# One plain pair of feed-forward columns fewer in each of three stages, with VectorE making those units' low parts in two of them

## The reference

```python
def swiglu(x, w_gate, w_up, w_down):
    return (jax.nn.silu(x @ w_gate) * (x @ w_up)) @ w_down
h = h + 0.5 * swiglu(rmsnorm(h, norm), w_gate, w_up, w_down)   # widths 1024 -> 2816 -> 1024
```

## Time and profile before

| | |
|---|---|
| time, median of 3 | 1736.12 us (1735.33 to 1736.40) |
| profiled execution: own time / span | 1735.85 us / 1734.1 us |
| busy share of the span: PE / PEld | 99% / 85% |
| DVE / ACT / POOL | 67% / 50% / 45% |
| granted TensorE clock, mean | 0.997 |
| start of stage one / two / three on PE (first L620 of the stage) | 7.37 / 888.58 / 1372.9 us |

### The profile page before, as it was taken

How to read it: one execution, slowest core, us unless ns; L and a number is a source line. 1 busy time by engine, 2 the same in 40 slices (tenths; PEclk the granted TensorE clock), 3 DMA queues, 4 the chain that set the end, 5 groups by cost and what they waited for, 6 DMA issues and landing times.

```text
span 1734.1 us, 28483 instructions
## 1 busy us (share of the span) xinstructions
PE 1720.6 (99%) x10096; PEld 1475.9 (85%) x10096; DVE 1156.5 (67%) x1709; ACT 870.9 (50%) x1486; POOL 782.8 (45%) x423
## 2 busy tenths in 40 slices
PE   9999999999999999999999999999999999999998
PEld 7899988888888777788888999988866889999887
DVE  6887874278867885236469877743786598787532
ACT  6455552266554477785344555522425445555322
POOL 2344354467565433325453344544533534435443
PEclk9999999999999999999999999999999999999998
DMA  5333333333333221112323333333362323333332
GB/s 178 98 103 104 108 101 95 128 95 88 110 110 113 63 72 50 50 50 85 98 92 94 107 107 101 108 97 98 103 146 62 97 85 101 105 109 110 97 97 74
DMA packets 50519, 168.56 MB, mean 97 GB/s; under 512 B 6264, under 2 KB 7032, under 8 KB 50304
## 3 DMA queue, kind: packets, MB, share of 16 engines
q1 hardware_dynamic: 47088, 161.34, 31.0%
q10 hardware_dynamic: 3344, 6.05, 1.2%
HBM read 161.84 MB, written 2.11 MB: 95 GB/s over the span
## 4 chain that ended last, share of the span: by engine, by line
PE 93%; DVE 3%; issue 2%; ACT 1%; POOL 1%; DMA 0%; POOLq 0%; SPq 0%; ACTq 0%
PE bank L620 16%; PE bank L621 16%; PE bank L622 16%; PE bank L734 8%; PE bank L735 8%; PE bank L732 8%; PE bank L914 8%; PE bank L746 3%; PE bank L959 2%; PE bank L985 2%; PE bank L1087 1%; PE bank L976 1%; PE bank L744 1%; DVE input_low L1691 1%; DVE tile L1708 1%
## 5 line engine op out<-in xcount | busy, mean ns | idle before, releaser
L487 POOL TENSOR_TENSOR weights_low<-raw_weights,weights_high 128x1024 fp32r<-128x1024 f32 x192 | 470.2, 2453 | 559.5 <-ACT weights_high L1204 531.0
L1204 ACT CAST weights_high<-raw_weights 128x1024 fp32r<-128x1024 f32 x244 | 254.7, 1048 | 295.0 <-DMA raw_weights<-weights 277.2
L528 POOL TENSOR_TENSOR weights_low<-raw_weights,weights_high 128x512 fp32r<-128x512 f32 x100 | 149.5, 1516 | 285.1 <-DVE weights_low L1844 285.1
L620 PE MATMUL bank<-input_high,weights_high 128*128 128x512 f32 x624 | 246.2, 395 | 2.8 <-DVE input_low L1691 2.1
L622 PE MATMUL bank<-input_low,weights_high 128*128 128x512 f32 x624 | 243.1, 390 | 0.0
L621 PE MATMUL bank<-input_high,weights_low 128*128 128x512 f32 x624 | 243.1, 390 | 0.0
L734 PE MATMUL bank<-input_mixed,weight_sum_low 128*128 128x256 f32 x600 | 169.7, 283 | 0.0
L735 PE MATMUL bank<-input_mixed,weight_sum_high 128*128 128x256 f32 x600 | 169.6, 283 | 0.0
L732 PE MATMUL bank<-input_mixed,weight_sum_high 128*128 128x256 f32 x600 | 169.5, 282 | 0.0
L735 PE MATMUL bank<-input_mixed,weights_high 128*128 128x256 f32 x600 | 169.4, 282 | 0.0
L732 PE MATMUL bank<-input_mixed,weights_high 128*128 128x256 f32 x600 | 169.1, 282 | 0.0
(11 more groups left out here) (322 smaller groups left out, 4139.7 us busy)
## 6 DMA issues: line engine op xcount, KB each, us to landing
raw_weights<-weights SPq DMA_DIRECT2D x294, 512.0 KB, 3.6
out_t<-out_t SPq DMA_DIRECT2D x8, 256.0 KB, 2.2
residual<-x_t SPq DMA_DIRECT2D x6, 256.0 KB, 6.2
glu_stacked<-glu_padded ACTq DMA_DIRECT2D x24, 64.0 KB, 4.5
glu_stacked<-glu_padded SPq DMA_DIRECT2D x24, 64.0 KB, 4.4
mem_in<-mem_t ACTq DMA_DIRECT2D x1, 1024.0 KB, 4.8
tile<-forget_sums ACTq DMA_DIRECT2D x4, 256.0 KB, 3.3
raw_weights<-weights SPq DMA_DIRECT2D x3, 256.0 KB, 6.2
```

Of the source, the lines that this page charges most:

```text
L487: pool.tensor_tensor(wl[:, u % RING, :], raw[:, u % RING, :], wh[:, u % RING, :].bitcast(F32), ALU.subtract).then_inc(low_done, 1)
L528: pool.tensor_tensor(wl[:, u % RING, w], raw[:, u % RING, w], wh[:, u % RING, w].bitcast(F32), ALU.subtract).then_inc(low_done, 1)
L620: pe.matmul(out, wh[:, u % RING, w], rh, start=start, stop=False)
L1204: act.copy(wh[:, u % RING, :], raw[:, u % RING, :]).then_inc(high_done, 1)
```

## The change

Plain pairs go from 6, 5, 5 to 5, 4, 4, so that 17, 18 and 18 pairs are mixed. With an even number of plain pairs the mixed pairs use banks 6/7 and 0/1 in turn (`pair_bank`), so the first product need not wait for a plain pair to be emptied; the down product's first unit goes through the banks in an order that fits. In stages two and three VectorE makes the low parts of units 2 to 7 (`weight_low`), and GpSimd makes none of the plain ones. `sums` is issued inside the first pair, two chunks before its end, and the factor is spread one chunk earlier. The seven combinations of the input are stored in another order, and for chunks 2 and 3 they are rounded and subtracted in two pieces (the first 3, then the last 4); the first product waits for the first pieces, the wide product of the first mixed pair for the last ones. ScalarE's order loses the two `high`s and the `silu` of the pair that is gone. TURN_1S is only renamed.

```diff
-PLAINS = {"g1": 6, "g2": 5, "g3": 5}
+PLAINS = {"g1": 5, "g2": 4, "g3": 4}
+EARLY, LATE = slice(0, 3), slice(3, 7)
-ND_OF, E_OF, NF_OF, NG_OF, B21, B22, B11, B12 = range(8)
+B11, E_OF, NG_OF, B21, ND_OF, B22, NF_OF, B12 = range(8)
...
+        def pair_bank(name, p):
+            n = PLAINS[name]
+            return 2 * ((n + p) % 2) if n % 2 else 6 * (p % 2 == 0)
...
 # GpSimd, gate_up_lows
-                for u in range(first, u0 + 2 * plain):
+                for u in range(first, 0 if u0 else 2 * plain):
                     low_part(u)
                 next_quarter(0)
...
 # TensorE, pair_start: in the loop over k, not behind it
-                if name != "ffn1":
-                    sums(name)
+                    if k == (DK if name in ("ffn2", "ffn3") else DK + 2) and name != "ffn1":
+                        sums(name)
 # TensorE, gate_up
-                    project(u0 + 2, ..., inside=lambda: spread_factor(feed), behind=1)
+                    project(u0 + 2, ..., inside=lambda: spread_factor(feed), behind=0)
 # TensorE, first_product
-                pe.wait_ge(sem("xmix_low"), before(name, 4) + 4)
-                pe.wait_ge(sem("ff_hidden"), before(name, FC) + plain - 1)
+                pe.wait_ge(sem("xmix_low"), before(name, 6) + 4)
+                if plain % 2:
+                    pe.wait_ge(sem("ff_hidden"), before(name, FC) + plain - 1)
                 pe.wait_ge(sem("quarter_low"), pairs_before(name, 1) + 1)
 # TensorE, mixed_pair, ahead of wide_product
+                if p == 0:
+                    pe.wait_ge(sem("xmix_low"), before(name, 6) + 6)
 # ScalarE, gate_up, stages two and three
                     high(u0 + 7)
-                    mixed_input(2)
-                    if plain > 4:
-                        high(u0 + 8)
-                    mixed_input(3)
+                    mixed_input(2, EARLY)
+                    mixed_input(2, LATE)
+                    mixed_input(3, EARLY)
+                    mixed_input(3, LATE)
                     silu(2)
-                    if plain > 4:
-                        high(u0 + 9)
-                        silu(3)
 # VectorE
+            def weight_low(u):
+                dve.wait_ge(high_done, u + 1)
+                dve.tensor_tensor(wl[:, u % RING, :], raw[:, u % RING, :], wh[:, u % RING, :].bitcast(F32),
+                                  ALU.subtract).then_inc(low_done, 1)
 # VectorE, factor(name, u0)
                     total_squares(name)
+                if u0:
+                    weight_low(u0 + 2)
                 inverse(name)
+                if u0:
+                    weight_low(u0 + 3)
 # VectorE, gate_up, the order of stages two and three after it
+                    plain_taken(0)        mixed_input(0)
+                    weight_low(u0 + 4)    plain_hidden(0)    mixed_input(1)
+                    weight_low(u0 + 5)    mixed_input_low(0, 1)
+                    plain_taken(1)        plain_hidden(1)    mixed_input(2)
+                    weight_low(u0 + 6)    mixed_input_low(1, 2)
+                    mixed_input(3)        weight_low(u0 + 7)
+                    mixed_input_low(2, 3, EARLY)    mixed_input_low(3, 5, EARLY)
+                    mixed_input_low(2, 5, LATE)     mixed_input_low(3, 6, LATE)
+                    plain_taken(2)        frame(-1)          plain_hidden(2)
+                    plain_taken(3)        plain_hidden(3)
 # VectorE, the order of stage one after plain_hidden(1), mixed_input(2), mixed_input_low(1)
+                    plain_taken(2)    mixed_input(3)
+                    the same four pieces of mixed_input_low
+                    plain_hidden(2)   plain_taken(3)    plain_hidden(3)   frame(-1)

```

More of the change, by code:

```diff
@@ L711, in gate_up @@
                 else:
-                    project(u0 + 2, bank[2][:, :], xh, xl, u0 + 3, inside=lambda: spread_factor(feed), behind=1)
+                    project(u0 + 2, bank[2][:, :], xh, xl, u0 + 3, inside=lambda: spread_factor(feed), behind=0)
                     project(u0 + 3, bank[3][:, :], xh, xl, u0 + 4)
@@ L766, in mixed_pair @@
                 plain, mixed = PLAINS[name], FC - PLAINS[name]
-                up, gate, b = u % RING, (u + 1) % RING, 2 * ((plain + p) % 2)
+                up, gate, b, after = u % RING, (u + 1) % RING, pair_bank(name, p), pair_bank(name, p + 1)
                 first, second = slice(0, HALF), slice(HALF, S)
@@ L786, in mixed_pair @@
                     pe.wait_ge(sem("ff_hidden"), at(before(name, FC) + plain + p, 1))
-                    mixed_product(bank[2 - b][:, first], wh[:, (u + 2) % RING, 0:S], quarter_low, B11
+                    mixed_product(bank[after][:, first], wh[:, (u + 2) % RING, 0:S], quarter_low, B11
                                   ).then_inc(sem("products"), 1)
@@ L800, in down @@
                     spread_unit(u0 + f, hidden_high(f), hidden_low(f), u0 + f + 1,
-                                first=(4, 5, 6, 7, 0, 1, 2, 3) if f == 0 else (), held=(0, "ff_hidden", before(name, FC) + FC))
+                                first=() if f else (4, 5, 6, 7, 0, 1, 2, 3) if PLAINS[name] % 2 else (2, 3, 4, 5, 6, 7, 0, 1),
+                                held=(0, "ff_hidden", before(name, FC) + FC))
                 with pe.Fori(0, 2) as i:
@@ L1325, in silu, with mixed_input @@
                     act.activation(tiles[c % 2][:, :], tiles[c % 2][:, :], ACT.Silu).then_inc(sem("ff_silu"), 1)
-                def mixed_input(k):
+                def mixed_input(k, part=slice(0, 7)):
                     act.wait_ge(sem("xmix_made"), before(name, 4) + k + 1)
-                    act.copy(xmix[k][:, :, 0:HALF], xsum[k % 3][:, 0:7, :]).then_inc(sem("xmix_high"), 1)
+                    act.copy(xmix[k][:, part, 0:HALF], xsum[k % 3][:, part, :]).then_inc(sem("xmix_high"), 1)
                 def copy_product(dst, src, at):
@@ L1344, in at @@
                         return n if i is None else i * (2 * step) + n
-                    b = bank[2 * ((plain + p) % 2)]
+                    b = bank[pair_bank(name, p)]
                     act.wait_ge(unit_done, at(u0 + 2 * (plain + p) + 2, 2))
@@ L1410, in gate_up @@
                     high(8)
-                    mixed_input(2)
+                    mixed_input(2, EARLY)
                     high(9)
+                    mixed_input(2, LATE)
+                    mixed_input(3, EARLY)
+                    mixed_input(3, LATE)
                     silu(2)
-                    high(10)
-                    mixed_input(3)
                     silu(3)
-                    high(11)
-                    silu(4)
                 frame(-1)
-                copy_product(copies[:, 0, 0, :], bank[2 * (plain % 2)][:, 0:HALF], 1)
+                copy_product(copies[:, 0, 0, :], bank[pair_bank(name, 0)][:, 0:HALF], 1)
                 silu(plain - 1)
@@ L1857, in gate_up @@
                 mixed_input(0)
-                if not u0:
-                    plain_taken(1)
-                plain_hidden(0)
-                mixed_input(1)
-                mixed_input_low(0)
-                if u0:
-                    plain_taken(1)
-                plain_hidden(1)
-                mixed_input(2)
-                mixed_input_low(1)
-                if not u0:
-                    plain_taken(2)
-                mixed_input(3)
-                if u0:
-                    plain_taken(2)
@@ L1873, in gate_up @@
-                mixed_input_low(2)
-                plain_hidden(2)
-                if not u0:
-                    plain_taken(3)
-                mixed_input_low(3)
-                if not u0:
-                    plain_hidden(3)
-                for c in range(3 if u0 else 4, plain - 1):
-                    plain_taken(c)
-                    plain_hidden(c)
-                frame(-1)
+                if u0:
+                    weight_low(u0 + 4)
+                    plain_hidden(0)
+                    mixed_input(1)
+                    weight_low(u0 + 5)
+                    mixed_input_low(0, 1)
+                    plain_taken(1)
+                    plain_hidden(1)
+                    mixed_input(2)
+                    weight_low(u0 + 6)
+                    mixed_input_low(1, 2)
+                    mixed_input(3)
+                    weight_low(u0 + 7)
+                    mixed_input_low(2, 3, EARLY)
+                    mixed_input_low(3, 5, EARLY)
+                    mixed_input_low(2, 5, LATE)
+                    mixed_input_low(3, 6, LATE)
+                    plain_taken(2)
+                else:
+                    plain_taken(1)
+                    plain_hidden(0)
+                    mixed_input(1)
+                    mixed_input_low(0, 1)
+                    plain_hidden(1)
+                    mixed_input(2)
+                    mixed_input_low(1, 2)
+                    plain_taken(2)
+                    mixed_input(3)
+                    mixed_input_low(2, 3, EARLY)
+                    mixed_input_low(3, 5, EARLY)
+                    mixed_input_low(2, 5, LATE)
```

(9 more changed lines are left out.)

36 lines of the change are left out of this document (16 added, 20 removed).

## The result

The changed kernel takes 1740.61 us (median of 11; 1739.37 to 1742.94) beside 1735.76 us (median of 11; 1734.73 to 1736.98) for the kernel before on the same chip: ratio 1.0027, 95% interval 1.0019 to 1.0036, so 4.85 us slower. The profiled execution is the slowest of the eleven, 1742.94 us with a span of 1741.1 us, 7.0 above the span of before; its mean granted clock is 0.994. Since it is 2.3 us above the median, its rows show the mechanisms, and sizes are taken from the medians as well.

What follows compares the result with a forecast made beforehand. PE was taken as the bound, 93% of the chain. Terms of -2.61, -2.02 and +6.4 us gave +1.8 on 1736.12, so 1737.9 us; the forecast's own range was 1735.9 to 1739.9, the whole range 1731.2 to 1743.5.

Steps and rivals of the forecast that it cites:

- the rival that was given 0.19: Stages two and three: the stall also halves PE's clock, losing 1.6 to 3.2 us each; 1741.1 to 1744.3 us; chance 0.19.
- Term 1: All three stages: one plain pair each becomes mixed, 10.88 to 10.01 us on PE, saving 2.61 us in all.
- Term 2: Squares' sums in stages two and three: earlier total and sums end a 1.01 us wait in each, saving 2.02 us.
- Term 3: First mixed product in stages two and three: PE waits 3.2 us each for GpSimd's quarter low part, adding 6.4 us.
- The rival without a stall: First mixed product, stages two and three: quarter in time, 1731.5 us, or 1734.7 with half stalls; no or little stall 0.29.
- VectorE's low parts: Units 6 and 7: low parts come late, PE waits there instead, time stays 1738 us; rival's chance 0.04.

Runs made afterwards that it cites:

- gate_ahead: reordered, with VectorE emptying the gate bank of plain pair 3 ahead of the up bank of pair 2: 1732.37 us, ratio 0.9979.
- sums_and_stage_one: Kernel before with five plain pairs in stage one only, squares' sums inside the first pair, VectorE making low parts of units 2 and 3: 1732.60 us.
- sums_late: Changed kernel with the squares' sums issued behind the first pair again, two chunks later, in stages two and three: 1740.28 us, ratio 1.0026.
- gpsimd_lows: Changed kernel with GpSimd making the plain units' low parts again in stages two and three, VectorE none: 1750.5 us, ratio 1.0086.
- high_early: Changed kernel with ScalarE's rounding of unit 8 moved from behind silu(2) to behind mixed input 2, stages two and three: 1733.14 us, ratio 0.9986.
- experiment 10: Changed kernel unaltered, run again for a second profile: 1740.31 us, ratio 1.0025; the profiled execution took 1740.61 us.
- warm: Changed kernel with 13 extra, unused 512-column matmuls on PE ahead of the quarter wait in stages two and three: 1737.98 us, ratio 1.0011.
- frame_first: high_early, with the first mixed pair's weight sums ahead of the third plain pair on VectorE and silu(2) behind them on ScalarE: 1736.58 us, ratio 1.0002.
- stage_one_alone: Kernel before with five plain pairs instead of six in stage one, nothing else: 1734.55 us, ratio 0.9995.
- reordered: high_early, with ScalarE's first product copy ahead of the last weight sum's rounding and VectorE's up half of plain pair 2 behind the sums: 1734.19 us.

## Why the prediction came out as it did

The time, 1740.61, lies 2.7 us above the forecast of 1737.9, outside the forecast's own 1735.9 to 1739.9 and inside the whole range only because that took in rivals on both sides. What happened is the rival that was given 0.19, at a time just under its 1741.1 to 1744.3; slower by over 0.2% had 0.29, no change 0.44.

**Term 1** (2.61 us) was right as far as it can be told: with term 2 it is contained in gate_ahead, and its stage one part with term 2 in sums_and_stage_one (3.2 measured, 2.89 worked out). The profiles of the kernel before and of the changed one show its part in the later stages too. In stage two, from the first mixed product to the start of stage three the kernel before takes 429.02 us and the changed one, without its slow matmuls, 438.99, so the extra mixed pair costs 9.97, forecast 10.01. Stage one has no wait; its first mixed product starts at 62.98, forecast 63.2.

**Term 2** (2.02 us) was right in size and in its reason, a total that comes early because GpSimd rests. The wait went (no bracket at 897.00), and the adds take 2.13 us, forecast about 2.2. The earlier place of the sums, with which the prediction opens this term, adds nothing: sums_late shows that, and gpsimd_lows that with GpSimd working the earlier place lengthens the wait, from 1.01 to 2.30 us (start to start). The Trainium skill, SBUF — State Buffer, section "SBUF: two separate sides", has VectorE, when both of its inputs lie in SBUF, and GpSimd share a port pair which one of them holds for a whole instruction. The traces agree: 6.39 and 6.43 us beside GpSimd's low parts, 2.13 without.

**Term 3** (two stalls of 3.2 us) was right in mechanism and size: 3.42 and 3.41 us lost, 28.57 us of VectorE's queue for 28.6, the quarter as releaser. What made it right was to sum the other engine's queue row by row instead of counting only what PE saves. high_early shows the cause: one `high` moved ahead of one silu and that stall is gone.

**The step that failed** is the clock, which the forecast left at 2.4 GHz behind the stall and priced only in a rival. The argument against that rival was that a stall of 3.2 us is shorter than the sparse end of the kernel and has dense work on both sides. Neither held. The sparse stretch was read as longer than it is: there the clock falls at 1724.9, when PE has not waited at all and its last 512-column matmuls are 0.6 us old (last section). And dense work on both sides did not keep the clock up: in the first profile it fell before PE resumed (0.90 in 930.50 to 934.20), in the second one just after (experiment 10). In the rival the price was 1.6 to 3.2 us in each stage. The profiles show 2.87, 2.63, 1.60 and 1.63, and on the median warm shows 1.3 per stage, less than the rival's low end. That the fall lasts "once or twice as long as the stall" was an assumption that came out: about 3 and about 6 us of slow work behind stalls of 3.4. The Trainium skill, TensorE: Matmul & The Clock Gate, section "HAM oscillation", says that a wait between groups of matmuls can leave the next group cold; here the trace agrees, 0.50 behind a wait of 3.26 us.

With that term the sum closes: -4.63 + 6.83 + 2.6 = +4.8, measured +4.85. The last term is itself a difference of medians, so what this tests is that warm lies 2.2 us above the kernel before, where 2.15 was measured. That it agrees to 0.05 is partly luck, since the traces have 0.7 us outside the terms and the kernel's end varies by more than that (last section).

**The rival without a stall** would have given 1731.5. high_early and gate_ahead reach 1733.1 and 1732.4: a changed order of the same work was enough for most of it, but each order has a next late link.

**VectorE's low parts** came in time; that rival did not occur.

## What to carry to other kernels

Taking work off the bounding engine moves it towards everything that used to be in time: before removing it, sum the queue of the engine that feeds the next stage, from start to start, and compare arrival times; if the feed loses, first look for a step on it that stands behind something it does not need. A wait of some 3 us on TensorE should be priced with slow matmuls behind it; whether they matter is quickly tried with filler matmuls. And of two engines that disturb each other, giving the work to the busier one can be the faster choice.

## What the runs showed of the hardware that was not expected

**The clock falls at a wait of some 3 us, sometimes while PE still waits and sometimes after it has resumed, and not each time.** In the changed kernel it fell at waits of 3.24 to 3.26 us in all four stages profiled. In one profile it fell before PE resumed and stayed low for 6 us of work; in the other it fell after 0.3 us of work in stage two and after 1.1 in stage three, and stayed low for about 3. In sums_late the wait of 3.2 us in stage two left no trace and the one in stage three did. Windows of sums_late:

```profile
934.00:937.00 3.00, 3.00 (x20) 2.69 (x21) 3.00 (x6) 1.60 (x3) 0.16 (x1) 1.00 0.00 0
...
1420.00:1423.00 3.00, 3.00 (x15) 2.81 (x14) 3.00 (x6) 1.59 (x3) 0.33 (x1) 0.56 0.00 0
```

**Equal waits, unequal clocks.** In frame_first PE waited 2.13 us between dense groups, and the clock stayed at 1.00. In gpsimd_lows it waited 2.14 us ahead of the squares' sums, eight matmuls of one column which take 0.9 us, and the clock fell 0.7 us behind them, at about 900.7. Windows of frame_first, then of gpsimd_lows:

```profile
938.00:943.00 5.00, 2.87 (x22) 2.51 (x22) 4.83 (x8) 3.53 (x7) 1.51 (x1) 1.00 0.34 107
```
```profile
896.00:900.80 4.80, 2.66 (x16) 2.06 (x15) 3.19 (x3) 0.61 (x2) 2.50 (x1) 0.99 0.37 109
900.80:904.00 3.20, 3.20 (x10) 2.55 (x9) 0.00 (x0) 1.88 (x2) 2.36 (x1) 0.50 0.19 28
```

In the kernel before, a wait of 0.84 us stands ahead of the same sums and the clock stays at 1.00. Whether the thin matmuls behind the wait made the difference, or only the moment of the wait, is open: no run tested it alone, and the median of frame_first suggests that other executions of it did not keep the clock. Nor is it settled why the clock returned after 3 us in some executions and after 6 in others.

**The clock also falls where PE does not wait.** Near the end of every kernel stand 24 matmuls of one column, then three of 512 and 16 of 128 columns. Timeline of PE at the end of the kernel before with a window of it, then of high_early:

```profile
1720.91 2.73 PE L1170 MATMUL bank<-ones,tile 128*128 128x1 f32 x24
...
1725.62 1.91 PE L1190 MATMUL bank<-identity,token_root 128*128 128x128 f32 x8
```
```profile
1720.00:1724.80 4.80, 4.80 (x36) 4.33 (x35) 1.23 (x3) 1.33 (x3) 0.00 (x0) 1.00 0.00 0
```
```profile
1718.70 2.73 PE L1180 MATMUL bank<-ones,tile 128*128 128x1 f32 x24
...
1723.06 1.06 PE L1200 MATMUL bank<-identity,token_root 128*128 128x128 f32 x8
```

In the kernel before PE is busy all the time; the clock is at 1.00 up to 1724.80 and at 0.50 from 1725.00, in the middle of this work; in high_early the clock stays up until it is done. From the first of the 24 matmuls to the end of the span it takes 12.6 us in high_early, frame_first, sums_and_stage_one, gate_ahead, gpsimd_lows and stage_one_alone, 13.0 to 13.2 in both profiles of the changed kernel and that of the kernel before, 13.4 in reordered, 13.5 in sums_late and 13.8 in warm. So up to 1.2 us of a difference between two profiles here comes from the end of the kernel, whatever the change, and differences of a few tenths between the experiments should not be read as theirs.
